# Compression phase of an NSA + SSD layer pair: heads innermost in the arrays, weight sums on VectorE, ten products ordered by feature halves

## What is computed

```python
kc = rms_norm(compress_blocks(full_c[:, :, 0], cmp_pe[0], cmp_w1[0], cmp_w2[0]), qk_gain[1])
vc = compress_blocks(full_c[:, :, 1], cmp_pe[1], cmp_w1[1], cmp_w2[1])
```

## Time and profile before

| what | us |
|---|---|
| median of three runs | 2580.79 |
| the profiled execution | 2583.15 |
| its span | 2581.7 |
| TensorE matmul busy | 2290.2 (89%) |
| VectorE busy | 1449.5 (56%) |
| GpSimd busy | 892.2 (35%) |
| first and last start of a compression product (L921) | 217.9 and 669.0 |

### The profile page before, as it was taken

One profiled execution on the slowest core, in us unless ns is written; L12 is line 12 of the kernel. 1 busy time (PEld: TensorE's weight loads), 2 busy tenths in 40 slices (PEclk: granted clock), 3 DMA queues, 4 the chain that ended last, 5 costly groups with the idle time before them and its releaser, 6 DMA issues.

```text
span 2581.7 us, 34092 instructions
## 1 busy us (share of the span) xinstructions
PE 2290.2 (89%) x12134; PEld 1816.8 (70%) x12134; DVE 1449.5 (56%) x2229; ACT 511.4 (20%) x1184; POOL 892.2 (35%) x796
## 2 busy tenths in 40 slices
PE   7989966987778865899998999999878899999899
PEld 6857755876655643788886888788544687888687
DVE  4456777666267821455576226877676526557522
ACT  1201010110245732021110003232354001111000
POOL 3433115111200036524443324555364335433232
PEclk9997988888778987899999999999788899999999
DMA  3313223222310169621211221222132121121122
GB/s 153 112 52 126 66 66 106 66 66 78 108 31 1 34 207 338 247 76 72 98 66 45 90 110 59 79 83 82 71 131 99 52 95 66 66 98 66 46 89 80
DMA packets 75159, 237.11 MB, mean 92 GB/s; under 512 B 11281, under 2 KB 44178, under 8 KB 60658
## 3 DMA queue, kind: packets, MB, share of 16 engines
q1 hardware_dynamic: 61826, 188.28, 20.3%
q0 software_dynamic: 13168, 46.68, 5.4%
HBM read 218.46 MB, written 23.73 MB: 94 GB/s over the span
## 4 chain that ended last, share of the span: by engine, by line
PE 55%; DVE 7%; issue 3%; ACT 3%; POOL 2%; DMA 2%; POOLq 1%; DVEq 0%; ACTq 0%; SPq 0%
PE ps L342 45%; PE ps L1410 1%; DMA sbuf<-w_nsa_out 1%; PE ps L1454 1%; POOL sbuf L2999 1%; ACT sbuf L1517 1%; PE ps L1434 1%; PE ps L467 1%; ACT sbuf L1525 1%; DVE sbuf L2382 1%; PE ps L1385 1%; POOLq L1708 1%; PE ps L2572 1%; DVE sbuf L2140 1%; DVE sbuf L2135 1%
## 5 line engine op out<-in xcount | busy, mean ns | idle before, releaser
L342 PE MATMUL ps<-sbuf 128*128 128x272 f32 x6048 | 1420.6, 398 | 52.6 <-DVE sbuf L2140 19.4
L342 PEld LDWEIGHTS ps<-sbuf 128*128 128x128 f32 x6048 | 1161.2, 193 | 310.0 <-issue 25.2
L392 POOL TENSOR_TENSOR sbuf<-sbuf 128x512 f32<-128x512 f32 (+2 forms) x90 | 136.7, 1519 | 734.0 <-PE ps L342 619.3
L921 PE MATMUL ps<-sbuf 128*128 128x256 f32 (+1 forms) x1280 | 305.8, 400 | 14.8 <-POOL sbuf L1160 10.7
L361 ACT ACTIVATE sbuf<-ps 128x272 f32<-128x272 f32 x180 | 71.5, 397 | 1155.2 <-PE ps L342 1125.8
L921 PEld LDWEIGHTS ps<-sbuf 128*128 128x128 f32 x1280 | 250.2, 197 | 66.8 <-issue 16.7
L372 DVE TENSOR_TENSOR sbuf<-sbuf,ps 128x272 f32<-128x272 f32 x90 | 39.4, 437 | 238.3 <-PE ps L342 237.2
L781 POOL DMA_DIRECT2D sbuf<-cmp_pages x128 | 68.9, 539 | 273.0 <-issue 267.0
L399 POOL TENSOR_TENSOR sbuf<-sbuf 128x512 f32<-128x512 f32 (+2 forms) x90 | 145.7, 1618 | 7.8 <-PE ps L342 1.0
L396 POOL TENSOR_TENSOR sbuf<-sbuf 128x512 f32<-128x512 f32 (+2 forms) x90 | 139.9, 1555 | 7.1
L393 POOL TENSOR_TENSOR sbuf<-sbuf 128x512 f32<-128x512 f32 (+2 forms) x90 | 138.4, 1538 | 7.1
(11 more groups left out here) (358 smaller groups left out, 2589.6 us busy)
## 6 DMA issues: line engine op xcount, KB each, us to landing
sbuf<-w_gu SPq DMA_DIRECT2D x44, 1024.0 KB, 5.7
sbuf<-w_down SPq DMA_DIRECT2D x32, 704.0 KB, 5.4
sbuf<-w_ssd_in SPq DMA_DIRECT2D x20, 1024.0 KB, 4.8
sbuf<-cmp_pages POOLq DMA_DIRECT2D x128, 128.0 KB, 4.6
sbuf<-cmp_pages SPq DMA_DIRECT2D x128, 128.0 KB, 3.3
sbuf<-w_nsa_in SPq DMA_DIRECT2D x10, 1024.0 KB, 5.9
sbuf<-sel_k SPq DMA_DIRECT2D x64, 128.0 KB, 2.8
sbuf<-sel_v SPq DMA_DIRECT2D x64, 128.0 KB, 3.8
```

The lines of the kernel that those rows point to most:

```text
L342: last = pe.matmul(ps[:, bank_of(u, j), 0:HALF], a[:, kt * P:(kt + 1) * P], b[:, kt], start=kt == 0, stop=kt == kts - 1)
L392: do(pool.tensor_tensor(sv[:, 0], a21, a22, ALU.add), f_sums)
L921: last = pe.matmul(product_of(u, j, ht), w[:, kt * 256 + ht * P:kt * 256 + (ht + 1) * P], moving[:, kt], start=kt == 0, stop=kt == KT - 1)
```

## The change

The diff, cut to what matters; the page rows are reordered on the host so that the group runs innermost, and every view of them follows:

```diff
@@ p1_dve
-                if u == NORM_UNIT:
-                    transform(dve, do, 0, 0)
+                if u == 8:
+                    transform(dve, do, 0, T_MID)
+                    weigh(dve, do, 0, T_MID)
@@ layout
+        stage = xT_flat[:, 3200:4224]
-            return buf[:, 0:n * 256].rearrange("p (i x r c) -> p r x i c", i=n, x=HK, r=4), n, slice(lo, lo + 2 * n)
+            return buf[:, 0:n * 256].rearrange("p (i r y) -> p r i y", i=n, r=4), n, slice(lo, lo + 2 * n)
-            return 10 * u + 2 * j + ht
+            return 10 * u + 5 * ht + j
-            return T_all[:, j, 0:HK * groups_of(u)].rearrange("p (x n) -> p x n", x=HK)
+            return T_all[:, j, 0:HK * groups_of(u)].rearrange("p (n x) -> p n x", x=HK)
-            return hidden[:, ht, 0:GROUPS * 4 * groups_of(u)].rearrange("p (g n r) -> p r g n", g=GROUPS, r=4)
+            return hidden[:, ht, 0:GROUPS * 4 * groups_of(u)].rearrange("p (n r g) -> p r n g", g=GROUPS, r=4)
-            return hidden[:, ht, 0:GROUPS * 4 * groups_of(u)].rearrange("p (g n) -> p g n", g=GROUPS)
+            return hidden[:, ht, 0:GROUPS * 4 * groups_of(u)].rearrange("p (n g) -> p g n", g=GROUPS)
@@ p2_pe
-                moving = t_of(u, j).rearrange("p (g k) n -> p k g n", g=GROUPS)
+                moving = t_of(u, j).rearrange("p n (k g) -> p k n g", g=GROUPS)
...
-                for j in range(5):
-                    for ht in range(2):
+                for ht in range(2):
+                    for j in range(5):
                         products(u, j, ht)
...
+                        if (ht, j) == (0, T_MID) and u >= 1:
+                            if u == PAIRS + 1:
+                                prompt_spread()
+                            second(pe, u - 1)
+                        if (ht, j) == (0, T_LAST) and u == 0:
+                            bias_product(0)
+                        if (u, ht, j) == (NU - 1, 1, T_SUM):
+                            cmp_scores(pe, 0)
+                        if u == PAIRS:
+                            if (ht, j) == (0, T_LAST):
+                                bias_product(1)
+                            if (ht, j) == (0, T_DIFF):
+                                key_sums()
+                            if (ht, j) == (1, T_LAST):
+                                key_spread(0)
+                                key_spread(1)
+                            if (ht, j) == (1, T_SUM):
+                                key_spread(2)
+                                key_spread(3)
@@ p2_act
+            def prompt_rows_on(kv):
+
+                act.wait_ge(prompt_in, 16 * 8 * (kv + 1))
+                if kv:
+                    act.wait_ge(rows_read[0], PAIRS)
+                src = stage.rearrange("p (i g y) -> p g i y", i=PPAGES, g=GROUPS)
+                dst = rows_a[:, NPAGE * 256:].rearrange("p (i y g) -> p g i y", i=PPAGES, g=GROUPS)
+                for g in range(GROUPS):
+                    do(act.activation(dst[:, g], src[:, g], ACT.Copy), c_turn)
...
+                if u in (2, PAIRS + 1):
+                    prompt_rows_on(u // PAIRS)
                 take_mid(u, 0)
...
+                take_sum(u, 0)
...
+                take_mid(u, 1)
+                hide(u, 0)
                 take_sum(u, 1)
-                hide(u, 0)
@@ p2_dve
+        def weigh(dve, do, kv, j):
+
+            if j == T_MID:
+                raw_there(dve, kv)
+            if kv:
+                dve.wait_ge(c_mm, product_at(PAIRS - 1, j, 1) + 1)
+            elif j == T_DIFF:
+                dve.wait_ge(c_turn, 32)
+                dve.wait_ge(stored, 16)
+            else:
+                dve.wait_ge(f_mm, multiplied(8 if j == T_MID else 9, 6))
+            if j == T_MID:
+                do(dve.scalar_tensor_tensor(w_of[j], w_raw[1], 2.0, w_raw[0], ALU.mult, ALU.add), c_w)
+            else:
+                do(dve.tensor_tensor(w_of[j], w_raw[1], w_raw[0], ALU.add if j == T_SUM else ALU.subtract), c_w)
...
             for u in range(NU):
                 if u == 0:
                     for j in (T_FIRST, T_LAST, T_SUM, T_DIFF):
+                        if j in (T_SUM, T_DIFF):
+                            weigh(dve, do, 0, j)
                         transform(dve, do, 0, j)
                 else:
                     transform(dve, do, u, T_DIFF)
                     if u <= PAIRS:
                         take_k(u - 1)
+                    if u == PAIRS:
+                        weigh(dve, do, 1, T_DIFF)
                     if u == PAIRS + 1:
                         key_scale(PAIRS)
-                take_outer(u, T_FIRST)
+                take_outer(u, T_FIRST, 0)
+                take_outer(u, T_LAST, 0)
+                four_outputs(u, 0)
                 if u + 1 < NU:
                     transform(dve, do, u + 1, T_MID)
-                take_outer(u, T_LAST)
+                take_outer(u, T_FIRST, 1)
+                if u == PAIRS:
+                    key_roots()
+                if u == PAIRS - 1:
+                    weigh(dve, do, 1, T_MID)
                 if u + 1 < NU:
                     transform(dve, do, u + 1, T_FIRST)
...
+                take_outer(u, T_LAST, 1)
...
                 four_outputs(u, 1)
...
+                if u == PAIRS - 1:
+                    weigh(dve, do, 1, T_SUM)
                 if u + 1 < NU:
                     transform(dve, do, u + 1, T_SUM)
@@ p2_pool
-            raw_there(pool, 0)
-            pool.wait_ge(f_mm, multiplied(8, 6))
-            sum_mid()
             pool.wait_ge(f_mm, multiplied(9, 6))
-            sum_sum()
+            load_rows(pool, 1, 1)
             pool.wait_ge(in_ev, 20)
             pool.wait_ge(hs_out, 12)
             pool.dma_start(t["out_kv"], kvT).then_inc(stored, 16)
-            load_rows(pool, 1, 1)
             prompt_rows(0)
-            pool.wait_ge(c_turn, 32)
-            pool.wait_ge(stored, 16)
-            sum_diff()
             for u in range(2, NU):
                 pool.wait_ge(rows_read[1], u)
                 load_rows(pool, u, 1)
-                if u == PAIRS:
+                if u == 3:
                     prompt_rows(1)
-                    raw_there(pool, 1)
-                    for j, do_sum in ((T_MID, sum_mid), (T_SUM, sum_sum), (T_DIFF, sum_diff)):
-                        pool.wait_ge(c_mm, product_at(u - 1, j, 1) + 1)
-                        do_sum()
@@ p3_pe
-            cmp_scores(0)
+            scores(0)
             for k in range(4):
                 cmp_turn(0, k)
```

More of the change, by code:

```diff
@@ L906, in products @@
                 if j in (T_MID, T_SUM):
-                    taken = c_act, 4 * u + 2 * (j == T_SUM) + ht + 1
+                    taken = c_act, 4 * u + 2 * ht + (j == T_SUM) + 1
                 else:
-                    taken = c_dve, 6 * u + {T_FIRST: 0, T_LAST: 2, T_DIFF: 4}[j] + ht + 1
+                    taken = c_dve, 6 * u + 3 * ht + {T_FIRST: 0, T_LAST: 1, T_DIFF: 2}[j] + 1
                 claim(pe, c_bank(u, j, ht), *taken)
@@ L925, in p2_pe @@
             for u in range(NU):
-                for j in range(5):
-                    for ht in range(2):
+                for ht in range(2):
+                    for j in range(5):
                         products(u, j, ht)
-                        if u == PAIRS and j == T_DIFF and ht == 0:
-                            key_spread(2)
-                            key_spread(3)
-                    if j == T_MID and u >= 1:
-                        if u == PAIRS + 1:
-                            prompt_spread()
-                        second(pe, u - 1)
-                    if u == 0 and j == T_LAST:
-                        bias_product(0)
-                    if u == PAIRS and j == T_FIRST:
-                        bias_product(1)
-                    if u == PAIRS and j == T_LAST:
-                        key_sums()
-                    if u == PAIRS and j == T_SUM:
-                        key_spread(0)
-                        key_spread(1)
+                        if (ht, j) == (0, T_MID) and u >= 1:
[17 more added lines that the diff above has]
+                                key_spread(3)
             pe.wait_ge(c_mm, 10 * NU)
@@ L994, in hide @@
                 act.wait_ge(c_pre, 2 * u + ht + 1)
-                do(act.activation(by_positions(u, ht), by_positions(u, ht), ACT.Silu,
-                                  bias=cbias[:, 2 * kv + ht:2 * kv + ht + 1]), c_hid)
+                act_on = hidden[:, ht, 0:GROUPS * 4 * groups_of(u)]
+                do(act.activation(act_on, act_on, ACT.Silu, bias=cbias[:, 2 * kv + ht:2 * kv + ht + 1]), c_hid)
             def take_bias(kv):
@@ L1021, in p2_act @@
                     take_bias(0)
+                if u > PAIRS:
+                    take_v(act, do, u - 1)
+                take_sum(u, 0)
                 if u == PAIRS:
@@ L1144, in p2_dve @@
                     key_scale(1)
-                four_outputs(u, 0)
+                if u + 1 < NU:
+                    transform(dve, do, u + 1, T_LAST)
```

(23 more changed lines are left out.)

79 lines of the change are left out of this document (24 added, 55 removed).

## The result

The changed kernel took **2538.38 us** (median of 4 runs, 2534.83 to 2541.17), the kernel before 2580.78 beside it: ratio 0.9833, 95% interval 0.9816 to 0.985. It is faster by 1.7%, 1.4 us above the forecast and inside the range. In the last set of experiments it took 2542.31 us against 2577.72: 0.9855, 0.9832 to 0.9879. The gain is thus 42.4 us in one set and 35.4 in the other, where the forecast had 44: that the first came within 1.4 us is in part luck.

The account below looks back on a forecast made before the run. A ring through VectorE and the loads, not TensorE, was taken to bound the key units. Compression -29, before it -5.8, behind it -9.3: total -44, profiled 2583.15 to 2539, less 2.4 to the median: 2537 us, range 2510 to 2572.

Parts of the forecast that it names:

- Ring of units 1 to 3: Loop through VectorE and loads that sets the key units' T_DIFF periods; layout and order by halves save 6.9, 6.9, 7.0 us.
- Start: Compression's unit 0: `out_kv`, issued behind 16 page loads, lands late; VectorE waits 6 us before the DIFF sum, +5.2 us.
- Unit 4: Period of the compression's unit 4: GpSimd stall of 16.9 us goes; two sums and a 7 us weight wait come, -12.6.
- unit 5: Period of the compression's unit 5: `second(4)` still waits for `key_scale(4)`, so half the saving, -3.5 us.
- unit 6: Period of the compression's unit 6: TensorE still late from the wait for `key_scale(4)`, so only -1.5 us.
- Unit 7: Period of the compression's unit 7: 6.9 us from the loop through VectorE plus one us of TensorE's lateness, -8 us.
- After the last T_DIFF: Compression's end: nine products for eight and `cmp_scores(0)` among them, less 5 us of idle time, +6.2 us.
- `second`: TensorE's strided reads of `hidden`: 5.4 us a call for 3.84, +6 in the compression and +3 for `second(7)`.
- rival 1: `second` dearer: at 8.5 us a call 2556 to 2560, chance 0.14; at 17 us about 2629, chance 0.07.
- Before the compression: End of the projection: T_MID moved behind unit 8, VectorE operations no longer slowed by GpSimd's sum, -5.8 us.
- Behind it: From the last product through `cmp_turn` to the prompt scores: shorter waits, compressed scores moved ahead, -9.3 us.
- Rival 2: Compression: runs of four slow the ten products; at 1.15 times, time about 2560 us; chance 0.07, of which 0.02 slower.

Follow-up runs that it names:

- second pair: The kernel before and the changed kernel, neither edited, each profiled a second time in the last set of experiments: 2576.1 and 2543.7 us as profiled.
- experiment 2: Changed kernel with the old order of the ten products (both halves of each kind in turn), new layout kept: 2534.79 us, ratio 0.9825.
- experiment 4: Changed kernel with the store of kvT issued on GpSimd's queue ahead of unit 1's 16 page loads, as in the kernel before: 2537.89 us, ratio 0.9832.
- experiment 6: Changed kernel with the six weight sums back on GpSimd, DIFF's sum ahead of its prompt rows: 2550.56 us, ratio 0.9894.
- experiment 1: Changed kernel with `second` reading contiguous slices of `hidden` instead of elements 16 bytes apart (computes other keys and values): 2532.3 us, ratio 0.9815.
- experiment 9: Changed kernel with T_MID of unit 0 back behind unit 7 of the projection, MID sum still behind unit 8: 2541.88 us, ratio 0.9857.
- Experiment 7: Changed kernel with `cmp_scores(0)` and `scores(0)` back behind `second(7)`, `cmp_turn` between them: 2544.5 us, ratio 0.9867.

## Why the prediction was right, and where it was not

The total held by its mechanisms and by errors that cancelled.

- **Ring of units 1 to 3**, -6.9, -6.9, -7.0: measured -7.0, -6.8, -7.4; in the second pair -6.7, -8.4, -5.8. Right, and experiment 2 splits it as forecast in kind. VectorE's 0.45 us was 0.424 and T_LAST's 0.69 was 0.69.
- **Start**, +5.2: the wait was there (4.93 us) and the stage grew by 4.1 and 4.3. The step erred in taking the wait as lost in full: TensorE's bias product bounds the stretch, and experiment 4 won 1.9.
- **Unit 4**, -12.6: -13.9, in the second pair -14.4. (The terms that I gave for it add to -12.2.) The forecast wait of 7 us for the weights was 7.59. But the 16.9 for GpSimd was bought with the two sums and that wait: with the sums back, the unit is only 2.8 longer (experiment 6). The lock's price was right, the gain over it small.
- **Unit 5**, -3.5, and **unit 6**, -1.5: -0.8 and +1.0, in the second pair +4.6 and +0.3. This is the step that failed. The dearer `second`, a term of its own in my sum, explains little of it: `second(4)`, in unit 6, became 0.64 us dearer (7.70 for 7.06), and the stretch of unit 5 holds no call. I gave these units part of the ring's saving while TensorE was the bound. From 430.47 to 493.46 us it has the products of unit 4, the bias product, key sums and spreads, and it idles 7.9, all but 0.2 of it after 485.75. Then the order by halves puts all of the second `four_outputs`, T_SUM and T_DIFF between the last product and `key_scale(4)`, for which `second(4)` waited: 10.5 us in both profiles, more than the 8.60 before, and 7.3 with the order by kind. I had named that wait and let it shrink.
- **Unit 7**, -8: -7.0, in the second pair -5.7.
- **After the last T_DIFF**, +6.2: +10.0, in the second pair +8.8. The ninth product was counted. TensorE's idle time before `second(6)` did shrink, from 14.12 to 2.33 us, but it lies ahead of the last T_DIFF, in unit 7, and the 5 that I took off here had no place in this stage. The compressed scores cost 3.99 us among the products, not 7.3.
- **`second`**, 5.4 us a call for +6 and +3: keys cost 4.8 to 5.0, values 7.7. Here two sizes were wrong and the sum came out right. I took 3.84 us as the price before, but that call stood at a granted clock of 0.64, and with it the 0.94 ns a column of rival 1: contiguous keys take 2.57 us at full clock. Against the full clock's price the stride costs 1.86-fold with keys and 2.05-fold with values, so VectorE's 1.4 was too small for both. At half clock it costs 1.06 and 1.09-fold, and three of the four calls with values in the kernel before stood there (7.06 to 7.09 us). So `second(7)` became 0.65 us dearer and not 3. That experiment 1 gives 9 us back, as the term says, is luck. The Trainium skill (SBUF — State Buffer, note on SBUF cachelines) has the direction, and experiment 1 shows it: same counts, neighbouring elements, 4.58 for 7.72 us. It gives no size.
- **Before the compression**, -5.8: L561's waits fell from 12.3 to 6.5 us, exactly so. By experiment 9 the place of T_MID is worth nothing there, since its 2.5 us come off one wait and onto the other; the 5.8 is what VectorE's two operations lose beside GpSimd's sum, 8.1, less the 2.3 of the MID sum. The start moved by -1.7 and -5.0 in the two pairs. What lies between is the granted clock: both kernels run at half speed after the wait, and L561's eight products, 2.08 us at half and 1.14 at full clock, show when it ends:

```profile
190.92 2.08 PE L561 MATMUL ps<-sbuf 24*64 24x272 f32 x8 [5.27 <-DVE sbuf L656]
...
202.78 2.08 PE L561 MATMUL ps<-sbuf 24*64 24x272 f32 x8
...
208.55 1.14 PE L561 MATMUL ps<-sbuf 24*64 24x272 f32 x8
```

  Here it ends near 208 us, in the second profile of the same kernel near 200. The changed kernel's median start, 208.5, is 7.5 and 9.7 us before the two starts of the kernel before, so the gain there may well be above my 5.8, and the first profile an unlucky one; with two profiles of the kernel before that is not shown.
- **Behind it**, -9.3: -10.2 to `cmp_turn`, where the forecast has -7.8; what differs is `second(7)`. The -1.5 for earlier prompt scores lies in the last stage and can't be read there. Experiment 7 finds 4 to 5 us in the place of the scores.

Of the rivals, none decided. Rival 2 (dearer products) is excluded: 36.7 us for ten, and 378 ns an instruction as before. Rival 1 was half true: with values a call takes 7.7 of its 8.5 us, but most of that was paid before, at the half clock.

## What to carry to other kernels

A saving in a ring is worth its size only in the stages where that ring is the bound: list for each unit the work of the engine that would be next, and give the saving only above it. An order that brings the first half's results sooner brings the second half's later; where the other engine is the bound, that is a loss, and the two orders can stand in one kernel. Before forecasting that a wait shrinks, ask what it waits for: one of the two longest here, 10.5 us, waited for a semaphore count one higher than its bank needed. And before one row serves as a price, read the granted clock beside it: one form of `second` took 2.57, 3.84 and 4.71 us before the change, at 1.00, 0.64 and 0.50.

## What the runs showed of the hardware

- TensorE reading f32 elements 16 bytes apart, 32 instructions: as moving data (128 columns) 4.79 us for 2.57 at a granted clock of 1.00 and 4.99 for 4.71 at 0.50; as weights of 127 columns 7.72 (at 0.72 to 0.78) for 3.76 (at 1.00), and 7.70 for 7.06 at 0.50. The strided read takes the same time at both clocks, so its loss and the half clock's hardly add.
- ScalarE paid nearly twofold for the same stride on its input (Silu of 1024 elements, 2.17 for 1.15 us); VectorE 1.47-fold for single elements against runs of four (622 for 424 ns).
- Executions with the same work up to there differ by some 9 us in when a half-speed stretch ends (starts of the compression from 207.0 to 216.5 us in nine profiles, 5.5 us apart in two of one kernel). Whether what is won there is lost later is not shown: the second profile of the changed kernel was 5.5 us ahead at the first product and 9 us slower behind `cmp_turn`, but of two variants that start at 208.5 one takes 1881.3 us there and the other 1891.3.
